# The maxima of prompt attention reach the queries' operand by small transfers in place of a second turn

## What is computed

```python
s = jnp.einsum('bqhd,bkhd->bhqk', qi, k, preferred_element_type=jnp.float32) * scale
s = s + fi.transpose(0, 2, 1)[..., :, None] - fk_t[..., None, :]
mask = k_pos[None, :] <= pi[:, None]
s = jnp.where(mask, s, -jnp.inf)
p = jax.nn.softmax(s, axis=-1)
return jnp.einsum('bhqk,bkhd->bqhd', p.astype(v.dtype), v)
```

## Time and profile before

| | |
|---|---|
| median of 3 runs | 3805.12 us (3803.58 to 3810.42) |
| the profiled execution's own time | 3806.07 us |
| its span, first to last instruction | 3804.3 us |
| TensorE busy | 3636.2 us (96%), 19019 matmuls |
| VectorE, ScalarE, GpSimd busy | 1799.7 us (47%), 1682.0 us (44%), 1075.1 us (28%) |
| mean granted TensorE clock | 0.978 |
| prompt attention | from about 1803 to 2410 us of the span |
| in it, the copies of L1307 | 32, 0.576 us each |
| the reductions of L1380 | 32, 0.166 us each |

### The profile page before, as it was taken

One profiled execution on the slowest core, in us unless ns is written; L12 is line 12 of the kernel. 1 busy time (PEld: TensorE's weight loads), 2 busy tenths in 40 slices (PEclk: granted clock), 3 DMA queues, 4 the chain that ended last, 5 costly groups with the idle time before them and its releaser, 6 DMA issues. The chain is left out here.

```text
span 3804.3 us, 55783 instructions
## 1 busy us (share of the span) xinstructions
PE 3636.2 (96%) x19019; PEld 2947.1 (77%) x19019; DVE 1799.7 (47%) x3039; ACT 1682.0 (44%) x3417; POOL 1075.1 (28%) x764
## 2 busy tenths in 40 slices
PE   8999999999999999997899999799999999799999
PEld 6788888787878888886678778677777777588787
DVE  3134433332123543332545445388888888544433
ACT  4224433455223533443434444477777777321222
POOL 0011122310011223220110010277777777322200
PEclk9999999999999999998789999899999999899999
DMA  4233334333233334332410000599999999544422
GB/s 159 80 116 132 118 127 145 114 126 112 99 112 119 125 125 151 118 123 61 113 51 17 23 18 12 186 346 341 341 331 329 334 333 332 189 176 156 150 91 81
DMA packets 354282, 590.75 MB, mean 155 GB/s; under 512 B 44030, under 2 KB 90214, under 8 KB 354027
## 3 DMA queue, kind: packets, MB, share of 16 engines
q1 hardware_dynamic: 341874, 580.20, 44.8%
q10 hardware_dynamic: 11584, 5.13, 0.5%
q0 software_dynamic: 576, 2.10, 0.2%
HBM read 475.38 MB, written 111.96 MB: 154 GB/s over the span
## 5 line engine op out<-in xcount | busy, mean ns | idle before, releaser
L853 PE MATMUL prj_z_ps<-prj_w_hi,prj_h_hi 128*128 128x512 f32 x2312 | 924.2, 400 | 3.0 <-DVE prj_w_lo L677 2.9
L855 PE MATMUL prj_z_ps<-prj_w_hi,prj_h_lo 128*128 128x512 f32 x2312 | 902.5, 390 | 0.0
L854 PE MATMUL prj_z_ps<-prj_w_lo,prj_h_hi 128*128 128x512 f32 x2312 | 901.5, 390 | 0.0
L1724 POOL TENSOR_TENSOR sa_v_lo<-sa_v_raw,sa_v_hi 128x1024 fp32r<-128x1024 f32 x256 | 609.8, 2404 | 217.4 <-DVE sa_v_hi L1863 216.9
L855 PEld LDWEIGHTS prj_z_ps<-prj_w_hi,prj_h_lo 128*128 128x128 f32 x2312 | 434.5, 188 | 93.7
L853 PEld LDWEIGHTS prj_z_ps<-prj_w_hi,prj_h_hi 128*128 128x128 f32 x2312 | 435.4, 188 | 90.2 <-DVE prj_w_lo L677 6.1
L854 PEld LDWEIGHTS prj_z_ps<-prj_w_lo,prj_h_hi 128*128 128x128 f32 x2312 | 435.5, 188 | 84.9
L1857 DVE TENSOR_TENSOR sa_kT_lo<-sa_t_ps,sa_kT_hi 128x512 fp32r<-128x512 f32 x512 | 345.4, 686 | 140.8 <-ACT sa_kT_hi L1746 136.8
L1746 ACT CAST sa_kT_hi<-sa_t_ps 128x512 fp32r<-128x512 f32 x512 | 291.9, 590 | 120.0 <-PE sa_t_ps L2010 112.7
L2010 PE MATMUL sa_t_ps<-sa_ident,sa_k_raw 128*128 128x128 f32 x2048 | 300.7, 277 | 22.9 <-DVE sa_kT_lo L1857 15.5
L2010 PEld LDWEIGHTS sa_t_ps<-sa_ident,sa_k_raw 128*128 128x128 f32 x2048 | 241.6, 141 | 103.0 <-DVE sa_kT_lo L1857 30.8
(11 more groups left out here) (308 smaller groups left out, 5922.8 us busy)
## 6 DMA issues: line engine op xcount, KB each, us to landing
sa_k_raw<-in_cache_k_dram SPq DMA_DIRECT2D x512, 256.0 KB, 4.1
sa_v_raw<-in_cache_v_dram SPq DMA_DIRECT2D x512, 256.0 KB, 4.3
prj_w_raw<-in_w_main_dram SPq DMA_DIRECT2D x272, 256.0 KB, 4.0
z_scratch<-prj_z_sb SPq DMA_DIRECT2D x272, 256.0 KB
mo_mg<-z_scratch SPq DMA_DIRECT2D x51, 512.0 KB, 3.8
prj_cu<-extp_scratch SPq DMA_DIRECT2D x48, 256.0 KB
pa_raw<-z_scratch SPq DMA_DIRECT2D x12, 1024.0 KB, 10.3
prj_x_in<-in_x_all_dram SPq DMA_DIRECT2D x17, 512.0 KB, 3.7
```

The source lines that it names most:

```text
L853: pe.matmul(out, h_hi[:, slot_of(t), k], hi, start=(k == 0), stop=False)
L854: pe.matmul(out, h_hi[:, slot_of(t), k], lo, start=False, stop=False)
L855: mm = pe.matmul(out, h_lo[:, slot_of(t), k], hi, start=False, stop=(k == KC - 1))
L1724: pool.tensor_tensor(v_lo[:, w % 2, at], v_raw[:, w % RING, at], v_hi[:, w % 2, at].bitcast(F32), ALU.subtract).then_inc(vlo_ready, 1)
```

## The change

The maxima no longer pass through `q_aug` and a second transpose. `negate` writes them to a buffer of its own, `neg_max`, two groups deep, and ScalarE's queue issues four transfers for each group (`place`), one a tile: 128 partitions x one word of `neg_max` become 128 words in row 66 of `qA`. The rows 64 and 65 stay the ones of the first turn. `place` stands right behind `negate` in the order. The turns of a head go from 12 to 8; `max_set` counts 16 for each transfer, 64 for each group.

```diff
-    TURNS = 3 * GROUPS
+    TURNS = 2 * GROUPS
...
-        q_aug = m.sb("q_aug", [P, 2, T, AUG + 3])
+        q_aug = m.sb("q_aug", [P, 2, T, AUG])
...
+        neg_max = m.sb("neg_max", [P, 2, QG], F32R)
...
             do.negate(h, hh, 0)
-            do.turn(h, hh, 2 * GROUPS)
+            do.place(h, hh, 0)
...
                     if units and units[-1] == MAX_UNITS[g + 1][-1]:
                         do.negate(h, hh, g + 1)
+                        do.place(h, hh, g + 1)
...
                         if j == 2 * GROUPS + QG - 1:
                             do.negate(h + 1, 1 - hh, 0)
+                            do.place(h + 1, 1 - hh, 0)
...
-                if j == steps - 1 and (g < GROUPS - 1 or not last):
-                    following = (h, hh, 2 * GROUPS + g + 1) if g < GROUPS - 1 else (h + 1, 1 - hh, 2 * GROUPS)
-                    do.turn(*following)
...
-            pool.memset(q_aug[:, :, :, AUG:AUG + 2], 1.0).then_inc(consts, 1)
...
-                    else:
-                        act.copy(qA[HEAD_DIM:AUG, hh, at], t_ps[HEAD_DIM:AUG, c % 2, :]).then_inc(max_set, 1)
+
+                def place(self, h, hh, g):
+                    act.wait_ge(max_ready, h * GROUPS + (g + 1))
+                    for t in range(QG):
+                        at = slice((QG * g + t) * P, (QG * g + t + 1) * P)
+                        act.dma_start(qA[AUG - 1:AUG, hh, at].bitcast(F32), neg_max[:, g % 2, t:t + 1].bitcast(F32)).then_inc(max_set, 16)
...
-                    dve.tensor_reduce(q_aug[:, hh, tiles, AUG + 2], part_max[:, tiles, 0:g + 1], AX.X, ALU.max,
+                    dve.wait_ge(max_set, h * (GROUPS * QG * 16) + max(g - 1, 0) * (QG * 16))
+                    dve.tensor_reduce(neg_max[:, g % 2], part_max[:, tiles, 0:g + 1], AX.X, ALU.max,
                                       negate=True).then_inc(max_ready, 1)
...
                     if j == 0:
-                        pe.wait_ge(max_set, h * GROUPS + (g + 1))
+                        pe.wait_ge(max_set, h * (GROUPS * QG * 16) + (g + 1) * (QG * 16))
```

More of the change, by code:

```diff
@@ L1197, in pair_begins @@
                 self.pair = pair
-            past = decay = turn = maximum = negate = score = weigh = lambda self, *where: None
+            past = decay = turn = maximum = negate = place = score = weigh = lambda self, *where: None
         @block.sync
@@ L1323, in _ @@
             dve.wait_ge(decay_loaded, 16)
-            dve.wait_ge(consts, 12)
+            dve.wait_ge(consts, 11)
             class VectorPart(Part):
@@ L1400, in _ @@
         def _(pe):
-            pe.wait_ge(consts, 12)
+            pe.wait_ge(consts, 11)
             class TensorPart(Part):
@@ L1407, in past @@
                         pe.wait_ge(whole_ready, self.pair + 1)
-                        pe.wait_ge(max_set, h * GROUPS + 2)
+                        pe.wait_ge(q_low, h * GROUPS + GROUPS)
                         pe.matmul(t_ps[:, 1, 0:HEADS], later[:], whole[:], start=True, stop=True).then_inc(later_summed, 1)
                 def turn(self, h, hh, c):
-                    if c == 2 * GROUPS + 3 and hh == 0:
+                    if c == 1 and hh == 1:
                         pe.wait_ge(rest_ready, self.pair + 1)
                     if c < 2:
-                        pe.wait_ge(max_set, h * GROUPS)
+                        pe.wait_ge(q_low, h * GROUPS)
                     elif c - 2 < GROUPS:
                         pe.wait_ge(k_low, h * GROUPS + (c - 1))
-                    elif c - 2 < 2 * GROUPS:
+                    else:
                         pe.wait_ge(q_low, h * GROUPS + (c - 1 - GROUPS))
-                    else:
-                        pe.wait_ge(max_set, h * GROUPS + (c - 1 - 2 * GROUPS))
                     if c == 0:
@@ L1427, in turn @@
                         pe.wait_ge(q_prepared, h + 1)
-                    if c >= 2 * GROUPS:
-                        pe.wait_ge(max_ready, h * GROUPS + (c - 2 * GROUPS + 1))
-                    src = k_aug[:] if c < GROUPS else q_aug[:, :, :, 0:AUG] if c < 2 * GROUPS else q_aug[:, :, :, 3:AUG + 3]
+                    src = k_aug[:] if c < GROUPS else q_aug[:]
                     for t in range(QG):
```

## The result

The changed kernel takes 3871.57 us in the median of four runs (3865.90 to 3878.69), the kernel before 3805.72 on the same chip. The ratio is 1.0169, with a 95% interval of 1.0151 to 1.0188: slower by some 66 us. The forecast was 3808 us and its range ended at 3837.

A forecast was written before the change was run, and what follows sets the result against it. TensorE's queue was taken to bound prompt attention (busy 556 of 607 us). Boundaries -4.9, exponentials +1 and clock +7 gave +3: 3806.07 becomes 3809, 3808 us for the median; range 3795 to 3837.

The forecast's parts named there:

- The gap: Time from the end of the maxima's negation to the next group's first score: 3.0 us, from 2.7 to 9.0.
- The sum by boundaries, -4.9: Prompt attention's group boundaries, each 3.0 us minus its old gap, no lower than what can come back: together -4.9 us.
- "+1 us" on the exponentials: Scores into group 3 waiting for exponentials delayed 1.4 us by issues: fits by 0.3 us, misses slightly in four heads; +1 us.
- The clock, "+7": TensorE's granted clock halves after 2.2 us holes into group 1: five falls in six heads, 1.4 us each, +7.
- The second one: Rival: transfers land slower, gap 4.0 us, clock falls at up to fourteen places; 3832 to 3837 us, chance 0.28.
- The third (words one by one): Rival: each of the 128 words is its own piece, landing nears 7.8 us; 3955 us, chance 0.07.
- The first: Rival: the clock holds and the transfer is quick, 2.7 us in place of 3.0; 3796 us, chance 0.18.
- fourth: Rival: the change does nothing, because the stage is held elsewhere at the boundaries; chance 0.05.
- start of the stage: First score of prompt attention, under the first loads: 5.4 us in place of a gap of 2.2, +3.2.
- gaps into group 1: Boundary from group 0 to 1: +6.1 over six heads at full clock, +1.3 and -1.1 in two at half clock.
- gaps into group 2: Boundary from group 1 to 2 in eight heads: 3.0 us against an old gap of 3.0, no change.
- gains into group 3 and at head ends: Dropped turn's time comes back where other work covers the transfer: -10.6 us into group 3, -3.8 at head ends.

The follow-up runs named there:

- SyncE's issue with filled holes: Changed kernel with the four transfers issued from SyncE's queue and unused transposes ahead of the first score of groups 1 and 2: 3842.72 us, ratio 1.0092.
- without transfers: Changed kernel with no transfers and the maxima's subtraction left out, exponential input scaled by 0.125, so it does not compute the function: 3771.60 us, ratio 0.9899.
- the run with SyncE's issue: Changed kernel with the four transfers of a group issued from SyncE's queue in place of ScalarE's: 3853.39 us, ratio 1.0121.
- Filling the holes alone: Changed kernel with 24 unused transposes on TensorE ahead of the first score of group 1 and 14 ahead of group 2's: 3856.84 us, ratio 1.0131.

## Why the prediction was wrong

Three terms of the sum were mis-sized: the price of an issue and with it the gap, the wait of the scores on the exponentials, and the clock. The gains, and the landing of a transfer with nothing beside it, were right.

- **The gap, "0.05 to wake the scalar engine, 3 x 0.34 for the three before the last, 1.8 to land, 0.1 to wake TensorE, 3.0 us".** The landing was nearly right (2.0), the issue mis-sized: 0.62, so 3 x 0.62 and a gap of 3.92. Of two rows I took the mean of seven issues to DRAM over an issue from SBUF to SBUF, 0.64 us, whose length I put down to the load beside it. It was a row of the same kind, and it came within 0.02. It was not "the one transfer" of that kind: the one ahead of it had 1.24. The gather, which I had not counted, lengthens the gap in three heads by 1.0 to 1.3 us; the head with the loads has 7.9 us, where I took 5.4; and at the start it was 10.4 us, not 5.4.
- **The sum by boundaries, -4.9.** The gains into group 3 (-10.6) and at the head ends (-3.8) were sized right: -10.4 and -3.1 appear where nothing holds the exponentials (SyncE's issue with filled holes), and -10.5 and -3.7 without transfers. In the changed kernel both are eaten. The boundaries into groups 1 and 2, which I had at +6.3 and 0, cost 18.9 and 7.7 by their gaps alone.
- **"+1 us" on the exponentials.** This step named its own condition, and the condition came true: "If an issue took 0.64, this cover would be gone and sixteen boundaries would pay about 1 us each." 15 boundaries pay 1.0 each (15.5 us); with what it does to the clock there it is 18 to 24 us by the run with SyncE's issue. I gave the sentence, and then gave its case neither a rival nor a place in the range. It does not alone leave the range: the forecast of 3808 with 18 to 24 us on it is 3826 to 3832.
- **The clock, "+7", five falls of 1.4 us, only into group 1.** The direction was right, the size far too small: there are 16 more falls and 85 us more at 1.2 GHz, which at the 0.35 us of the prediction's own price are 30 us (an estimate). At a gap of 3.9 the holes into group 2 are 2.1 us as well, and behind late exponentials it falls ahead of group 3 too. The stage's mean went to 0.88, not "0.90 or so", and TensorE was busy 13 us longer with 128 instructions fewer. Filling the holes alone gave back 15 us.
- **The rivals.** The second one (landing slower, up to 3837) had the gap right, 4.0, by "issues of 0.5, landing of 2.4"; it left out the scalar engine's queue, and had 13 to 18 us for the clock. The third (words one by one) is out: 128 words landed much as a row did, in 2.0 and 1.7 us. The Trainium skill, "DMA: Bandwidth & Descriptors", Rules for kernel authors, puts a plain transfer with a rearranged access pattern 19 times behind the hardware's transpose; no run here has that transpose beside it. The first and fourth are out.

Put together, the prediction's terms with what the traces have for them:

| term, us | forecast | from the traces |
|---|---|---|
| start of the stage | +3.2 | +7.1 |
| gaps into group 1 | +6.3 | +18.9 |
| gaps into group 2 | 0 | +7.7 |
| gains into group 3 and at head ends (by the run without transfers) | -14.4 | -14.2 |
| scores waiting for exponentials | +1 | +15.5 |
| clock (85 us at 0.35, an estimate) | +7 | +30 |
| sum | +3 | +65 |

The timelines say 64.2. The clock misses by 23 us, the exponentials by 14.5, the gaps by 12.6 and 7.7 and the start by 3.9; no single one of them would have left the range. The sum is not fitted to the timelines, but it is no proof that the terms are separate. The same sum, with their own starts, gaps, waits and half-clock times, gives 42 us for SyncE's issue, 44 for the filled holes and 33 for both, where the timelines have 44.6, 46.1 and 29.5. In heads 0 and 4 the parts of the half clock at the loop's end and of the unused transposes were not taken apart.

## What to carry to other kernels

A transfer that replaces a turn through PSUM holds its issuing engine first and the reader second: price the issues in that engine's program order, and ask who stands behind them, before pricing the landing. Take the issue's price from the rows of the same kind (source and destination memory), even if there are only one or two (0.64 and 1.24 us here), and when a step's cover rests on such a price, carry the case without cover into the range. Where 4 us of other work stand between producer and reader, and the issue is on an idle queue, such a transfer cost next to nothing here and the turn it replaced was a gain (0.24%); where they don't, the turn was the cheaper of the two. No run sent the four tiles of a group with one issue, so whether one longer transfer would hold the engine less stays open.

## What the runs showed of the hardware that I had not expected

- The issue of a small transfer from SBUF to SBUF took 0.60 to 0.62 us of the issuing engine in the median, from ScalarE as from SyncE, for 128 words from a column to a row or a column and for 512 bytes from a row to a row. One of another shape took 1.24. Lists on two queues run side by side (1.1 and 1.4 us for two each), but then land in 2.5 us in the median, the last in 2.9, and not in 2.0.
- Unused transposes ahead of a late score made the kernel faster by 15 us, with the clock of the stage at 0.93 in place of 0.88. By the Trainium skill, "TensorE: Matmul & The Clock Gate", Part 1, activity is what releases the throttle, and this trace agrees: the clock fell 7 times in the stage and not 18.
- Where TensorE stood in 101 short stalls of 1.1 us at most, the granted clock was 0.70 over 829 us, though it was busy for 88% of the stretch. A busy share near that of the changed kernel (85%) says nothing of the clock that goes with it: at half clock the same 3656 matmuls were busy for 729 us and not 569, so a low clock raises the share by itself.
